# Prompt attention and sample attention in one stage of a decoder step

## The reference, cut to what matters

```python
def _sb_attend(q, k, v, mask, sb_bias):
    z = jnp.einsum('bqhd,bkhd->bhqk', q.astype(jnp.float32), k.astype(jnp.float32)) * (q.shape[-1] ** -0.5)
    z = z + sb_bias.astype(jnp.float32)[None, :, None, None]
    log_1m = jnp.where(mask, jax.nn.log_sigmoid(-z), 0.0)
    excl = lax.cumsum(log_1m, axis=3, reverse=True) - log_1m
    a = jnp.where(mask, jnp.exp(jax.nn.log_sigmoid(z) + excl), 0.0)
    return jnp.einsum('bhqk,bkhd->bqhd', a, v.astype(jnp.float32)).astype(q.dtype)
...
        k_past = jnp.take(cache_sb_k[l], page_table, axis=0).reshape(db, -1, N_HEADS_SB, HEAD_DIM)
        v_past = jnp.take(cache_sb_v[l], page_table, axis=0).reshape(db, -1, N_HEADS_SB, HEAD_DIM)
```

## Time and profile before

| what | us |
|---|---|
| median of 3 runs (2284.97 to 2289.49) | 2288.51 |
| the profiled execution | 2293.12 |
| its span, first to last instruction | 2291.3 |
| busy: PE, PEld, DVE, ACT, POOL | 1918.0, 1700.2, 894.1, 713.6, 383.2 |

### The profile page before, as it was taken

One profiled execution on the slowest core, in us unless ns is written; L12 is line 12 of the kernel. 1 busy time (PEld: TensorE's weight loads), 2 busy tenths in 40 slices (PEclk: granted clock), 3 DMA queues, 4 the chain that ended last, 5 costly groups with the idle time before them and its releaser, 6 DMA issues. The chain is left out here.

```text
span 2291.3 us, 41063 instructions
## 1 busy us (share of the span) xinstructions
PE 1918.0 (84%) x17210; PEld 1700.2 (74%) x17210; DVE 894.1 (39%) x969; ACT 713.6 (31%) x1064; POOL 383.2 (17%) x173
## 2 busy tenths in 40 slices
PE   4999996477777578777777849799999999999997
PEld 4999994354555456555555539789999999999997
DVE  5201103557566455455455564552222122122223
ACT  4101001456555455445445530221211112121122
POOL 2112101000076500000000021212112121121220
PEclk7999996788898899999999979899999999999999
DMA  4222208401111299999999950143334334333332
GB/s 134 76 86 102 86 39 327 154 19 56 51 42 38 67 294 356 341 332 336 352 341 333 342 196 1 55 147 140 134 113 147 127 110 146 128 128 135 120 109 105
DMA packets 172929, 363.57 MB, mean 159 GB/s; under 512 B 21009, under 2 KB 62610, under 8 KB 171666
## 3 DMA queue, kind: packets, MB, share of 16 engines
q1 hardware_dynamic: 168498, 285.51, 37.7%
q0 software_dynamic: 3904, 75.76, 9.1%
q10 hardware_dynamic: 400, 0.53, 0.1%
HBM read 330.48 MB, written 98.11 MB: 187 GB/s over the span
## 5 line engine op out<-in xcount | busy, mean ns | idle before, releaser
L1195 PEld LDWEIGHTS sa_kt<-ident,sa_k_in 128*128 128x128 f32 x1344 | 154.9, 147 | 153.1 <-DMA sa_k_in<-in_cache_sb_k 76.1
L1195 PE MATMUL sa_kt<-ident,sa_k_in 128*128 128x128 f32 x1344 | 177.3, 288 | 80.9 <-DMA sa_k_in<-in_cache_sb_k 41.0
L393 POOL TENSOR_TENSOR mlp_w_lo<-mlp_raw,mlp_w_hi 128x2048 fp32r<-128x2048 f32 x30 | 138.0, 4601 | 585.3 <-ACT mlp_w_hi L439 585.3
L552 DVE TENSOR_TENSOR xT<-xT,mlp_acc 128x1088 f32<-128x1088 f32 x64 | 82.5, 1289 | 278.7 <-PE mlp_acc L144 278.7
L1376 DVE COPY sa_kT<-sa_kt 128x1024 f32<-128x1024 f32 (+1 forms) x88 | 103.5, 1176 | 222.1 <-PE sa_kt L1195 222.1
L144 PE MATMUL mlp_acc<-n_hi,mlp_w_hi 128*128 128x272 f32 x1024 | 171.8, 290 | 21.0 <-POOL mlp_w_lo L120 16.3
L144 PE MATMUL mlp_acc<-mlp_h_hi,mlp_w_hi 128*128 128x272 f32 x1024 | 170.5, 288 | 4.0 <-DVE mlp_h_lo L548 4.0
L144 PE MATMUL mlp_acc<-n_lo,mlp_w_hi 128*128 128x272 f32 x1024 | 170.9, 289 | 0.0
L144 PE MATMUL mlp_acc<-n_hi,mlp_w_lo 128*128 128x272 f32 x1024 | 170.5, 288 | 0.0
L144 PE MATMUL mlp_acc<-mlp_h_hi,mlp_w_lo 128*128 128x272 f32 x1024 | 169.6, 287 | 0.0
L144 PE MATMUL mlp_acc<-mlp_h_lo,mlp_w_hi 128*128 128x272 f32 x1024 | 169.6, 287 | 0.0
(11 more groups left out here) (158 smaller groups left out, 3329.8 us busy)
## 6 DMA issues: line engine op xcount, KB each, us to landing
sa_k_in<-in_cache_sb_k SPq DMA_DIRECT2D x256, 256.0 KB, 5.6
sa_v_in<-in_cache_sb_v SPq DMA_DIRECT2D x256, 256.0 KB, 5.5
out<-in_cache_win_k POOLq DMA_DIRECT2D x16, 2040.0 KB, 8.9
out<-in_cache_win_v POOLq DMA_DIRECT2D x16, 2040.0 KB, 8.9
sa_k_in<-in_cache_win_k SPq DMA_DIRECT2D x80, 256.0 KB, 7.7
sa_v_in<-in_cache_win_v SPq DMA_DIRECT2D x80, 256.0 KB, 7.2
mlp_raw<-in_w_up SPq DMA_DIRECT2D x16, 1024.0 KB, 12.0
mlp_raw<-in_w_down SPq DMA_DIRECT2D x16, 1024.0 KB, 11.8
```

The costliest lines, as they stand in the source:

```text
L393: pool.tensor_tensor(out=ring.lo[:, n % 2, :], in0=ring.raw[:, n % 2, :], in1=ring.hi[:, n % 2, :].bitcast(F32), op=ALU.subtract).then_inc ...
L552: dve.tensor_tensor(in_banks(xT[:, c, :]), in_banks(xT[:, c, :]), acc[:, c % 2, :, 0:BW], ALU.add).then_inc(added, 1)
L1195: last = pe.transpose(kt_ps[:, c, j * P:(j + 1) * P], k_in[:, i % KS, j, c * P:(c + 1) * P], ident[:, :])
```

## The change

`prompt_stage` and `sample_stage` become `attention_stage`. It has 48 steps, and each engine's list takes in each step one sample unit and two prompt pieces. A sample unit is now the same unit of two batch rows: the 32 partitions of a pair of heads hold the queries of both rows, scores and values of the rows are accumulated in one bank, and gates, scan, product and softmax run once for both. A prompt piece has at most 512 keys; the 64 tasks make 96 pieces. All turns (keys, prompt weights, sample weights, outputs) go through one ring of three PSUM banks in an order written out in advance, and `emptier` names the engine that empties each: of keys banks 0 and 2 ACT, 1 and 3 DVE, each 512 columns wide.

```diff
-    KS, VS, WS = 4, 4, 5
+    STEPS = B // TWO * NU
+    SLAG = 3
+    KS, VS, WS = 4, 4, 4
...
+    for x, (g, q) in enumerate(tasks):
+        n = (q + 1) * P
+        mid = 0 if n <= CH else n // 2 // P * P
+        if mid:
+            pieces += [(x, mid, n, True, False), (x, 0, mid, False, True)]
+        else:
+            pieces.append((x, 0, n, True, True))
...
+    PLAG, TW = 3, 4
...
+    RING = 3
...
+    def use_keys(u, bb, c):
+        if u < STEPS and tiles[u % NU]:
+            use(("keys", u, bb, c), BY_DVE if c % 2 else BY_ACT)
...
+    def use_piece(m, h):
+        if 0 <= m < NP:
+            use(("piece", m, h), BY_DVE if task_kind(m) == DIL and h else BY_ACT)
...
+                def bank(key):
+                    i = ring_at[key]
+                    if i >= RING:
+                        wait_left(pe, uses[i - RING])
+                    return ring[:, i % RING, :]
```

TensorE's list of a step. `score(k)` waits for the gates or logits of unit k-1 and for the keys (k, 1, 2) and (k, 1, 3) to be out of their banks; `pr_score(m)` waits for the gates or logits of piece m-1:

```diff
+                for k in range(LAST):
+                    m = 2 * k
+                    if k < STEPS:
+                        score(k)
+                    turn_weights(k - SLAG)
+                    turn_keys(k + 1, 0, 0)
+                    turn_keys(k + 1, 0, 1)
+                    pr_score(m)
+                    pr_turn(m - PLAG, 0)
+                    turn_keys(k + 1, 0, 2)
+                    values(k - SLAG, 0)
+                    pr_turn(m - PLAG, 1)
+                    turn_keys(k + 1, 0, 3)
+                    pr_values(m - PLAG - 1)
+                    if finished(k):
+                        turn_outputs(k)
+                    turn_keys(k + 1, 1, 0)
+                    pr_score(m + 1)
+                    pr_turn(m + 1 - PLAG, 0)
+                    turn_keys(k + 1, 1, 1)
+                    values(k - SLAG, 1)
+                    turn_keys(k + 1, 1, 2)
+                    pr_turn(m + 1 - PLAG, 1)
+                    pr_values(m - PLAG)
+                    turn_keys(k + 1, 1, 3)
```

The lists of ACT and DVE (`pr_scan(m, 0)` waits for the gates of both heads; `gate`, `broken`, `pr_gate`, `pr_scan`, `pr_weight` concern SB units and pieces, `dilated`, `softened`, `exponent`, `pr_logit`, `pr_exponent`, `pr_soften` DIL ones):

```diff
+                    gate(k)
+                    weights_out(k - SLAG)
+                    key_part(k + 1, 0, 0)
+                    pr_gate(m, 0)
+                    piece_part(m - PLAG, 0)
+                    key_part(k + 1, 0, 2)
+                    pr_gate(m, 1)
+                    piece_part(m - PLAG, 1)
+                    exponent(k)
+                    pr_exponent(m)
+                    if finished(k):
+                        outputs(k)
+                    key_part(k + 1, 1, 0)
+                    pr_gate(m + 1, 0)
+                    piece_part(m + 1 - PLAG, 0)
+                    key_part(k + 1, 1, 2)
+                    pr_gate(m + 1, 1)
+                    piece_part(m + 1 - PLAG, 1)
+                    pr_exponent(m + 1)
...
+                    if finished(k):
+                        own_rows(k)
+                    dilated(k)
+                    key_part(k + 1, 0, 1)
+                    broken(k)
+                    pr_soften(m - 1)
+                    pr_outputs(m - PLAG - 2)
+                    pr_logit(m)
+                    pr_scan(m, 0)
+                    piece_part(m - PLAG, 1)
+                    key_part(k + 1, 0, 3)
+                    pr_scan(m, 1)
+                    pr_weight(m)
+                    softened(k)
+                    pr_outputs(m - PLAG - 1)
+                    key_part(k + 1, 1, 1)
+                    pr_logit(m + 1)
+                    pr_soften(m)
+                    pr_scan(m + 1, 0)
+                    piece_part(m + 1 - PLAG, 1)
+                    pr_scan(m + 1, 1)
+                    pr_weight(m + 1)
+                    key_part(k + 1, 1, 3)
```

`weights_out` becomes two ACT instructions of half the columns, one for each row. SP issues the sample loads alone, for unit x when unit x-2 has left its slot; the prompt's loads and stores move from SP to POOL's queue, which no longer scales (`pr_soften` on DVE) or reverses queries: a second table, `by_distance_up`, is written in `natural_stage` and read backwards in `pr_logit`. `xT` leaves SBUF during attention:

```diff
+                for c in range(KC):
+                    if keep is not None:
+                        sp.dma_start(keep[c * P:(c + 1) * P, :], src[:, c, :]).then_inc(src_kept, 16)
+                    if kept is not None:
+                        sp.dma_start(residual[:, c, :], kept[c * P:(c + 1) * P, :]).then_inc(res_in, 16)
...
+                if kept is not None:
+                    dve.wait_ge(res_in, 16 * KC)
...
+                        if j == len(pieces) - 1:
+                            dve.wait_ge(summed, len(pieces))
+                            dve.tensor_copy(fd_up[:, :], fd[:, ::-1]).then_inc(reversed_, 1)
```

More of the change, by code:

```diff
@@ new lines, in turn_keys @@
+                def turn_keys(u, bb, c):
+                    n = u % NU
+                    if u >= STEPS or not tiles[n]:
+                        return
+                    i = key_of[u, bb]
+                    if c == 0:
+                        pe.wait_ge(k_loaded[i % KS], k_landed[u, bb])
+                    to = bank(("keys", u, bb, c))
+                    for j in range(tiles[n]):
+                        last = pe.transpose(to[:, j * P:(j + 1) * P], k_in[:, i % KS, j, c * P:(c + 1) * P], ident[:, :])
+                    last.then_inc(turned, 1)
@@ L1252, in values @@
+                    last.then_inc(turned, 1)
+                def values(u, bb):
+                    if not 0 <= u < STEPS:
+                        return
+                    n, i = u % NU, valued_of[u, bb]
+                    if n in (0, 3) and bb == 0 and u:
+                        pe.wait_ge(owned, groups_out(u + SLAG + 1))
+                    wait_left(pe, ("weights", u))
+                    pe.wait_ge(v_loaded[i % VS], v_landed[u, bb])
                     count = tiles[n] + new[n]
-                    for i in range(count):
-                        rows = P if i < tiles[n] else TS
+                    for x in range(count):
+                        rows = P if x < tiles[n] else TS
@@ new lines, in pr_turn @@
+                def pr_turn(m, h):
+                    if not 0 <= m < NP:
+                        return
+                    if h == 0:
+                        if task_kind(m) == SB:
+                            pe.wait_ge(pr_weights, m + 1)
+                        else:
+                            x = m if ended(m) else m + 1
+                            pe.wait_ge(pr_softened, pr_ends(x))
+                    to = bank(("piece", m, h))
+                    for y in range(0, span(m), P):
+                        last = pe.transpose(to[:, y:y + P], take_pr[:, m % TW, h, y:y + P], ident[:, :])
+                    last.then_inc(turned, 1)
@@ L1309, in gate @@
                     if x > WS:
-                        former = [y for y in range(u) if kind[y % NU] == SB and sb_count(y) == x - WS][0]
-                        act.wait_ge(w_turned, former + 1)
-                    act.activation(take[:, x % WS, 0:w], s_ps[:, u % 2, 0:w], ACT.Sigmoid, scale=SCALE, bias=zb[:, 0:1])
-                    act.activation(stay[:, x % 2, 0:w], s_ps[:, u % 2, 0:w], ACT.Sigmoid, scale=-SCALE,
+                        act.wait_ge(turned, ring_at["weights", sb_unit(x - WS)] + 1)
@@ new lines, in pr_exponent @@
+                def pr_exponent(m):
+                    if not ended(m) or task_kind(m) != DIL:
+                        return
+                    x = pieces[m][0]
+                    r = x - HU
+                    act.wait_ge(pr_lowered, r + 1)
+                    for i, y in enumerate([y for y in (m - 1, m) if pieces[y][0] == x]):
+                        for h in range(2):
+                            z = take_pr[:, y % TW, h, 0:span(y)]
+                            last = act.activation(z, z, ACT.Exp, bias=low_pr[:, x % 2, h:h + 1], accum_out=den_pr[:, r, i, h:h + 1])
+                    last.then_inc(pr_exped, 1)
```

1032 lines of the change are left out of this document (514 added, 518 removed).

## The result

The changed kernel took 2232.7 us (median of 4 runs, 2231.76 to 2234.28); the kernel before, on the same chip, 2289.0 (2284.97 to 2290.04). The ratio is 0.9758 [0.9741, 0.9775]: 2.4% faster, where 5.0% was forecast (2175 us). The profiled execution, 2234.3 us (its span is 2232.7), is 55.2 above the 2179 that the sum gave for one.

A forecast was written before the change was run, and what follows sets the result against it. Transfers were taken to bound the sample stage, latency the prompt stage. Fused: 743 us of steps + 25 clock + 42 ends = 810 against 927, plus 3 elsewhere, giving 2175 us, 5.0% faster; range 2080 to 2285.

The forecast's parts named there:

- I take 22 before the first step: Start of the fused stage: 22 us before its first step; with 20 behind the last, 42, bounded by 30 and 65.
- A full step is 16.0 us: First half of the fused stage: a full step takes 16.0 us, of which DVE stands about 5.5.
- the walk: Following each engine's list through the fused stage's steps: 743 us for 48 steps, before the clock and the ends.
- The clock at 0.95: TensorE's granted clock in the fused stage: 0.95, costing 0.53 us a step, 25 us in all.
- the second half: Last 24 steps of the fused stage: full steps of 16.9 or 15.7 us, weighted 16.5; 187 us per row pair.
- DVE's wait before its first key bank: Sign in the profile after: DVE idle some 3 us before a step's first key bank.
- the table loads: ACT in the fused stage: about 40 more loads of 1.28 us; 0.6 us a step survives on the chain.
- Rival 1: Softer walls in the fused stage: DVE stands 3 us a step, not 5.5; steps of 13.5 us, 2055 us; chance 0.20.
- Rival 2: The ring of three PSUM banks makes it slower: at 1.6 us a use, 2367 us; chance 0.14.
- Rival 3: TensorE stays at 1.2 GHz in the fused stage, 21.8 us a step: 2453 us; chance 0.04.
- Rival 4: The two merged stages barely overlap: a step takes 18.4 us, the old time; chance 0.05.
- DMA share about 0.8: Sign in the profile after: the fused stage's DMA share is about 0.8, no longer full.

The follow-up runs named there:

- b: Changed kernel without ACT's loads of the samples' window bias; POOL sets the tile to zero instead: 2213.7 us.
- c: Changed kernel with POOL's first two groups of prompt loads issued only when the first key banks may be emptied: 2227.5 us.
- n: Changed kernel with each of ACT's eight window-bias loads split into two of 8 rows, one per head: 2223.2 us.
- q_fill_half: Changed kernel with three thrown-away matmuls before each score, and products of only the first two key blocks of each sample row: 2202.1 us.
- g_fill: Changed kernel with three matmuls before each score whose results are thrown away: 2223.9 us.
- the early key bank: Changed kernel with one line of DVE's list moved: a step's last key bank is emptied ahead of the second prompt scan and product: 2170.3 us.
- j_best_late: Changed kernel with the early key bank, sample values beside the prompt's, bias loads behind first key tiles, POOL's small tables ahead of its delayed prompt groups: 2161.4 us.

## Why the prediction came out at half the gain

The sign was right, the time lies in the range, and the mechanism was right in outline: both stages' holes were filled, DMA no longer binds in the steps, no engine came near the span. Two terms were mis-sized, and they took half of the gain.

- *"I take 22 before the first step"* failed: 53.4 us. It was read off the first score of the sample stage, as if the fused stage's start held only that stage's loads. It holds the prompt's too, and the bias loads, doubled in bytes, had a new form that only two packets at a time served. b, c and n show it. The upper bound of 65 for both ends did not hold either: they took 53.4 + 15.5 = 68.9.
- *"A full step is 16.0 us"* failed for the first half: 17.8 at the full clock in the step shown. Up to the turn of key (1,2) the prediction's prices sum to 10.2 us of TensorE (scores of two rows 1.74, weights 0.45, nine turns of four 4.05, two piece scores 1.4, values of two rows 1.74, piece values of four blocks 0.87), and it took 11.8 without a gap: scores of two rows took 1.85, not 1.74, values of a row 1.02 (604.79 to 605.81), not 0.87, a piece score 0.84 (602.93 to 603.77), not 0.70, and four turns 0.49 ahead of other turns and 0.53 to 0.59 ahead of a product, not 0.45. So TensorE's own list, not the ring as in the walk, set that turn; q_fill_half's step at this place is 0.87 shorter for a list cut by 0.88. Emptying that bank and the two gates behind it took 0.7 more than walked. Over the 24 steps g_fill, where no score is slow, gives the size: 397.1 us, 28 above the walk's 369, of which 21 in the 16 full steps (15.5 to 18.5, 17.3 on average) and 7 in the others. What its thrown-away matmuls add by themselves is in the 28.
- *The clock at 0.95* was 0.91 as the mean of the stage: 0.97 in the second half, 0.88 and 0.90 in the first. The walk found DVE's wall but let TensorE stand there for nothing. g_fill prices the fall at 21 us at the least, against 12.5 assumed for this half; these 8.6 and the 28 above are the 37.
- Right: DVE's wait before its first key bank (3.57 us seen, "some 3").
- Right as sums only, and in part by luck: the second half (16.9 and 15.7 a step in the walk, weighted 16.5; 386.5 with clock, 382.4 measured). Its full steps ran from 14.4 to 22.3 us, 17.2 on average, the other steps were 3 us shorter together than walked, and at a clock of 0.97 the clock's 12.5 paid for the rest; no run tests what sets these steps. So with the table loads: the sum had 0.6 us for them in each of 16 steps, 10 us, and taking them away gave 9.0, but half of it outside the full steps. There are 42 in the stage, 23 more than the two stages had before (19), not "about 40 more".
- Rival 1 (softer walls, 2055) was reached by no kernel; the early key bank softens the first half's only, and lands at the forecast, 2170 us. Rival 2, the ring, is real with two banks. Rival 3: the clock did not stay at 1.2 GHz, and the start of two kernels parts turns from products. In b_no_window_bias TensorE stood 30.7 us, the last 27 at a granted clock of 0.50, then did 32 turns and nothing else, and at 425.0 us, during them, the clock rose to 1.00: turns began 0.21 us apart, then 0.11, and the score behind them ran at the full clock. j_best_late shows the same. So turns do raise the clock, and the doubt that the rival drew from them falls. Rival 4 did not come.
- "DMA share about 0.8" was 0.71; the same work in 810 us would be 0.76, an estimate (0.71 x 869.5 / 810).

The start of b_no_window_bias, timeline of PE:

```profile
421.50 5.75 PE L1082 MATMUL at_ring<-ident,at_k_in 128*128 128x128 f32 x32 [30.68 <-DMA at_k_in<-in_cache_win_k]
428.56 1.92 PE L1099 MATMUL at_s<-at_kT,at_qd 128*32 128x512 f32 x16 [1.32 <-DVE at_zb L1573]
```

Table loads in ACT's timeline of the changed kernel, the answer to the earlier trace rows, here with no wait between:

```profile
940.35 1.28 ACT L1371 ACT_TABLE_LOAD   x1
941.65 0.72 ACT L1371 ACTIVATE at_take_pr<-at_take_pr,at_low_pr 128x512 f32<-128x512 f32 x1
...
944.38 1.28 ACT L1295 ACT_TABLE_LOAD   x1
945.67 0.69 ACT L1295 ACTIVATE at_take<-at_s,at_zb 128x512 f32<-128x512 f32 x1
```

The next activation begins 1.30 us after the load's start, 1.29 the second time, with no drain on top, as the prediction took it from the earlier trace rows.

## What to carry to other kernels

When two pipelines are fused by hand-written lists, look at the end of each step for a short instruction that the next step's first one needs, and put it ahead of whatever only the far side needs; here one line was worth about as much as the fusion itself (62 and 56 us). Price a burst by what stands beside it, not by a row where it stood among its like, and price a stand of TensorE by the clock it loses too: a cut that only lengthens the stand may give nothing. When a load's shape changes, ask over how many engines it is spread, and what is queued behind it.

## What the runs showed of the hardware

- A burst of 32-column products took 0.87 us ahead of products of the same tile shape, and 1.01 ahead of turns or of 64-column products, before the change and after it. From the last matmul of a burst to the first of the next the trace shows 0.20 us where the shape changes and 0.11 between turns. The Trainium skill (TensorEngine Tiling (Array Packing), Key Properties) says that changing the tiling mode drains TensorE; it gives no price. From these rows about 0.1 us is an estimate (1.01 less 0.87, 0.20 less 0.11).
- TensorE's granted clock fell to 0.5 after many, not all, of its stands of 2 to 5 us between bursts, and stayed at 0.96 to 0.98 on average where matmuls without any use filled them (g_fill). 32 turns of fp32 tiles by themselves, behind a stand of 30.7 us at 0.50, brought it to 1.00 (b_no_window_bias).
- A load with an outermost dimension of two ran two packets at a time. In the changed kernel the fourth key tile of each row, issued beside it, landed 28 and 30 us after its issue, most others after 6 to 11, while the DMA share was 0.57 to 0.79 (in j_best_late one came after 39): a transfer can be late on engines that are on average partly idle.
